# Where the ones-product over the squares stands in PE's order, in a two-layer diffusion trunk on one core

## The chip, the core and the metric

One core of a Trainium2 chip runs the whole program. The time is device microseconds from launch to end. Three timed runs of the kernel before gave 2468.21, 2466.99 and 2468.08 us, a median of 2468.08.
## What is computed

Two trunk layers run over 512 latent and 128 context tokens, 640 in all, with a model width of 1024:

```
mod = silu(cond) @ w_ada + b_ada;  sh1, sc1, g1, sh2, sc2, g2 = split(mod, 6)
h = rms_norm(x, norm1_g) * (1 + sc1) + sh1
z = h @ w_in                       # then four parallel mixers (two attentions, two gated scans)
x = x + g1 * (merged branches @ w_out)
h2 = rms_norm(x, norm2_g) * (1 + sc2) + sh2
x = x + g2 * conv_ffn(h2, w_up, conv_w, conv_b, w_down)
```

`rms_norm` divides each token by the root of the mean of its squares over the 1024 channels. The change touches the two norms only, and the way each is reached from the product in front of it.

## The kernel before

**Layout and precision.** Activations lie transposed: 8 tiles of 128 channels by 640 tokens, x in `XT`. A product in near-fp32 precision is made of three fp32r products: weights and activations are each split into a rounded part (`WHI`, `HH`) and a rest (`RING_split`, `HL`), and `block_product` (lines 795 to 801) issues hi times hi, hi times lo and lo times hi, each in two halves of 320 columns. ACT makes the rounded part of each block of weights (`out_unit`, `up_unit`, `down_unit`, `unit_hi`), DVE the rest (`out_lo`, `up_lo`, `down_lo`, `lo_z`). Every engine's program is written out by hand in its own block, in order; nothing but semaphores couples them. An instruction that waits holds everything behind it on its engine.

**Stages of a layer.** Norm 1, the input projection, the mixers, the merge, the output projection (8 output tiles, `G_OUT` + t, 8 products of 48 matmuls each), norm 2, the up projection with the convolution, the down projection (8 output tiles, `G_DOWN` + j, 132 matmuls each in two parts of 66, over one `Fori` loop of two passes of four tiles on PE), then norm 1 of the next layer.

**How a norm is reached.** For each output tile DVE adds the residual into x (`residual`, line 2411), ACT squares that tile (`square`, line 1378), and DVE adds the square into `SQ_SUM` (`add_square`, line 1986). The first seven squares go into `SQ_SUM`, the eighth stays apart. PE then multiplies both by a matrix of 1/1024 in plain fp32 (`mean_square`, through `wide`, lines 787 and 788): a first pair of matmuls reads `SQ_SUM`, a second pair, added onto it in the same PSUM buffer, reads the eighth square. ACT takes the inverse root with a Ln and an Exp (`inv_root`, lines 1370 and 1372). DVE's `normed` and ACT's `modulate` then make the eight tiles of h in turn: DVE scales a tile (2045 or 2042), ACT rounds it with the shift (1389, and for odd tiles 1398), DVE makes the rest (2032 or 2029, in `rest(k)`). PE's next product (`two_products`, which makes two output tiles at once, 12 matmuls per tile of h) takes the tiles as they come (`h_ready`).

**Late modulation.** The last four column blocks of `w_ada` in a layer are multiplied after the output projection: `late(n)` on PE (line 1209), a copy of each row by ACT (`late_row_out`, line 1794), a turn into columns on PE (`late_turn`, line 1217), and one addition on DVE (line 2435). In `normed` DVE does tiles 0 to 3, then that addition, then tiles 4 to 7.

**The next layer's first weights.** At the sixth output tile of the down projection (j = 6) DVE's list also has `lo_z(l + 1, 0)` and `lo_z(l + 1, 1)` (line 2064), the rests of the next layer's first two weight blocks. They wait for ACT's `unit_hi` (line 1417), and ACT waits with that for the first part of the last output tile (`EV_DOWN + 14`), since the block is written over weights which that part reads.

Of the kernel before, what the change touches and what calls it, by code (L numbers as in the profile page):

```python
# [8 lines left out]
ALU = mybir.AluOpType  # L9
# [280 lines left out]
def build(nc, A, O):  # L290
    ctx = ExitStack()
    with ctx:
# [476 lines left out]
        def _(pe):  # L769
# [3 lines left out]
            for l in range(DEPTH):  # L773
# [63 lines left out]
                def mean_square(which):  # L837

                    if which:
                        wait_taken(pe, l, G_OUT + 6)  # L840
                    elif l:
                        wait_taken(pe, l - 1, G_DOWN + 6)
                    n = 2 * l + which
                    pe.wait_ge(sq_added, 8 * n + 7)
                    wide(pair(MS_AT[n]), ONES, SQ_SUM, True, False)
                    pe.wait_ge(sq_ready, 8 * n + 8)
                    wide(pair(MS_AT[n]), ONES, SQ[1], False, True).then_inc(ms_ready, 1)

                mean_square(0)
# [350 lines left out]

                for t in range(8):
                    wait_room(pe, l, G_OUT + t)
                    lo_ready(U_OUT + t)
                    product(use(G_OUT + t)[0], *out_weights(t), m_hi, m_lo, KT, t % 2 == 0, None if t else m_ready)
# [17 lines left out]
                late(0)  # L1222
                late(1)
                mean_square(1)
# [100 lines left out]
                with pe.Fori(0, 2) as it:  # L1325
                    down_first(it)
                    for j in range(1, 4):
                        g = G_DOWN + j
                        wait_room(pe, l, g, it)
                        for h in range(2):  # L1330
                            lo_ready(U_DOWN + 2 * j + h, it * 8)
                            product(use(g)[0], *down_weights(2 * j + h), lambda k: D_HI[11 * h + k],
                                    lambda k: ZT_R[:, 11 * h + k, :], 11, True, None, h == 0, h == 1)

        @block.scalar
        def _(act):
# [17 lines left out]
            for l in range(DEPTH):  # L1354
# [418 lines left out]
                for t in range(8):  # L1773
                    wait_event(act, l, EV_OUT + t)
                    if t < 5:
                        out_unit(t + 3)
                    elif t == 5:
                        log_and_exp()
                        up_unit(0, 0, w=W_APART)
                    elif t == 7:  # L1780
                        up_unit(0, 1)
                    if t:
# [144 lines left out]
        def _(v):  # L1927
# [12 lines left out]
            for l in range(DEPTH):  # L1940
# [78 lines left out]
                def normed(which, first, last):  # L2019
# [18 lines left out]
                    for k in range(first, last):  # L2038
# [11 lines left out]
                        if k > first:  # L2050
                            rest(k - 1)
                    rest(last - 1)
# [364 lines left out]
                for k in range(KT):  # L2417
                    if k < 5:
                        out_lo(k + 3)
                    elif k == 5:  # L2420
                        up_lo(0, 0, w=W_APART)
                    wait_event(v, l, EV_OUT + k)
# [3 lines left out]
                    if k:  # L2426
# [5 lines left out]
                up_lo(1, 0)  # L2432
                normed(1, 0, 4)
                v.wait_ge(late_turned, l * 4 + 4)
                nv.tensor_tensor(MOD[:, 40:48, :], columns(LATE_COLUMNS, 0, 8), bc(COLS[:, C_BADA + 40:C_BADA + 48].rearrange("p (j o) -> p j o", o=1), 2),
                                 ALU.add).then_inc(late_mod, 1)
                v.wait_ge(late_mod, l + 1)
                normed(1, 4, 8)
# [110 lines left out]
                for j in range(KT):  # L2549
                    if j < KT - 1:  # L2550
                        down_lo(2 * j + 2)
                        down_lo(2 * j + 3)
                    wait_event(v, l, EV_DOWN + 2 * j + 1)
                    residual(G_DOWN + j, j, 40)
                    if l + 1 < DEPTH:
# [5 lines left out]
                        if j:  # L2561
# [110 lines left out]
```

## Time and profile before

| | |
|---|---|
| median of three timed runs | 2468.08 us |
| the profiled execution | 2467.62 us, span 2465.8 us |
| PE busy, share of span | 2367.4 us, 96% |
| DVE, ACT, POOL busy | 1488.1, 1016.8, 305.7 us |
| mean granted TensorE clock | 0.990 |

The profiled execution lies inside the range of the timed runs. Its own time is 1.8 us more than its span. PE is the engine whose time is nearly the whole span; what the other engines do costs something only where PE waits for it, which is in a few places, two of them in each layer in front of a norm's product. In the rows below a line of the timeline begins with the start in us from the span's start and the duration; "x2" says that two instructions in a row were merged; the brackets give how long the engine had been idle and whose instruction ended that. Consecutive instructions of DVE and ACT overlap in the records by about 0.1 us.

### The profile page before, as it was taken

The numbers are of one execution on the slowest core, as the hardware profiler recorded it, in microseconds if no ns is written. First come the engines' busy times: TensorE is split into PE (matmuls) and PEld (weight loads), VectorE is DVE, ScalarE is ACT, GpSimd is POOL, SyncE is SP. The second block draws the span as 40 slices with busy tenths as digits, with TensorE's granted clock in tenths as the row PEclk, the third lists the DMA queues.
The fourth block names the chain that finished last, engine by engine and source line by source line (L and its number), as shares of the span: only waits on it lengthen the run. The fifth ranks groups of instructions, "written<-read, shape, count | busy, mean of one in ns | idle before, by whom it ended". The sixth has DMA issues, their size and how long they took to land. (4 is left out here: it accounts for less than half of the span.)

```text
span 2465.8 us, 49600 instructions
## 1 busy us (share of the span) xinstructions
PE 2367.4 (96%) x21594; PEld 2209.7 (90%) x21594; DVE 1488.1 (60%) x2274; ACT 1016.8 (41%) x1408; POOL 305.7 (12%) x203
## 2 busy tenths in 40 slices
PE   5999999999999999999989999999999999999998
PEld 4999867888999899999989996688899989999998
DVE  4134476986744788883241436778775658888621
ACT  4245565222252555561243536642222544555410
POOL 0000000000000545530000000000000006555000
PEclk8999999999999999999999999999999999999999
DMA  8555211222245233333244431122222633332321
GB/s 274 184 175 167 59 31 49 55 55 55 64 144 180 80 86 86 85 104 91 75 145 129 120 103 52 33 55 54 56 59 81 219 93 85 86 86 75 104 80 66
DMA packets 326509, 239.32 MB, mean 97 GB/s; under 512 B 18272, under 2 KB 317344, under 8 KB 325024
## 3 DMA queue, kind: packets, MB, share of 16 engines
q1 hardware_dynamic: 317584, 211.32, 29.4%
q10 hardware_dynamic: 8720, 24.99, 3.0%
q8 instruction: 162, 2.65, 0.4%
q14 instruction: 43, 0.35, 0.0%
HBM read 220.68 MB, written 15.60 MB: 96 GB/s over the span
## 5 line engine op out<-in xcount | busy, mean ns | idle before, releaser
L798 PE MATMUL PS<-HH_split,WHI_split 128*128 128x320 f32 x1952 | 617.6, 316 | 11.0 <-DVE HL_split L2032 9.5
L800 PE MATMUL PS<-HH_split,RING_split 128*128 128x320 f32 x1920 | 595.7, 310 | 0.0
L799 PE MATMUL PS<-HL_split,WHI_split 128*128 128x320 f32 x1760 | 546.9, 311 | 0.0
L798 PEld LDWEIGHTS PS<-HH_split,WHI_split 128*128 128x128 f32 x1952 | 369.5, 189 | 22.9 <-issue 13.3
L2057 DVE TENSOR_TENSOR RING_split<-RING,WHI_split 128x1024 fp32r<-128x1024 f32 (+2 forms) x154 | 222.4, 1446 | 269.1 <-ACT WHI_split L1725 182.0
L800 PEld LDWEIGHTS PS<-HH_split,RING_split 128*128 128x128 f32 x1920 | 362.7, 189 | 0.0
L799 PEld LDWEIGHTS PS<-HL_split,WHI_split 128*128 128x128 f32 x1760 | 333.7, 190 | 0.3
L799 PE MATMUL PS<-ZT_split,WHI_split 128*128 128x320 f32 x1032 | 320.0, 310 | 0.0
L748 POOL TENSOR_TENSOR BIG<-HH_split,HL_split 128x640 f32<-128x640 f32 x8 | 14.3, 1822 | 1752.9 <-DVE HL_split L2029 1752.9
L2064 DVE TENSOR_TENSOR RING_split<-RING,WHI_split 128x1024 fp32r<-128x1024 f32 x52 | 62.2, 1223 | 229.6 <-ACT WHI_split L1417 229.2
L799 PEld LDWEIGHTS PS<-ZT_split,WHI_split 128*128 128x128 f32 x1032 | 194.7, 189 | 0.0
L1251 PE MATMUL PS<-BIG_split,WHI_split 128*128 128x320 f32 x576 | 178.0, 309 | 0.0
L798 PE MATMUL PS<-V_split,WHI_split 128*128 128x320 f32 x480 | 151.0, 315 | 2.0 <-DVE RING_split L2057 2.0
L800 PE MATMUL PS<-V_split,RING_split 128*128 128x320 f32 x488 | 151.5, 310 | 0.0
L1725 ACT ACTIVATE WHI_split<-RING 128x1408 fp32r<-128x1408 f32 x32 | 44.1, 1379 | 219.7 <-PE PS L800 167.6
L1250 PE MATMUL PS<-V_split,WHI_split 128*128 128x320 f32 x432 | 133.7, 309 | 0.0
L1661 ACT ACTIVATE WHI<-PS 128x640 f32<-128x640 f32 x48 | 33.8, 705 | 223.6 <-PE PS L800 223.2
L1575 ACT ACTIVATE BIG<-PS,NMX 128x768 f32<-128x768 f32 (+1 forms) x120 | 94.2, 791 | 62.8 <-DVE NMX L2160 62.8
L1251 PEld LDWEIGHTS PS<-BIG_split,WHI_split 128*128 128x128 f32 x576 | 108.1, 188 | 0.0
L2263 DVE COPY_PREDICATED BIG<-MASK,PS 128x640 f32<-128x640 uint8 x96 | 84.6, 881 | 34.8 <-PE PS L1130 34.6
L2160 DVE TENSOR_REDUCE NMX<-PS 128x1 f32<-128x768 f32 (+1 forms) x120 | 93.1, 817 | 18.7 <-PE PS L1013 14.5
L1624 ACT ACTIVATE WHI_split<-RING 128x1280 fp32r<-128x1280 f32 (+1 forms) x54 | 67.0, 1241 | 67.9 <-PE PS L800 67.9
(321 smaller groups left out, 5489.6 us busy)
## 6 DMA issues: line engine op xcount, KB each, us to landing
RING<-in_w_in SPq DMA_DIRECT2D x96, 512.0 KB, 4.0
RING<-in_w_up SPq DMA_DIRECT2D x88, 512.0 KB, 5.0
RING<-in_w_ada SPq DMA_DIRECT2D x80, 512.0 KB, 6.3
RING<-in_w_down SPq DMA_DIRECT2D x32, 384.0 KB, 3.5
RING<-in_w_in SPq DMA_DIRECT2D x40, 256.0 KB, 3.3
RING<-in_w_down SPq DMA_DIRECT2D x32, 320.0 KB, 3.9
RING<-in_w_out SPq DMA_DIRECT2D x16, 512.0 KB, 4.5
ZT<-in_w_ada SPq DMA_DIRECT2D x8, 1024.0 KB, 9.0
```

The costliest lines, as they stand in the source:

```text
L798: release(pe.matmul(out, w_hi, hi[:, a:b], start=begin, stop=False), fresh and a == 0)
L799: pe.matmul(out, w_hi, lo[:, a:b], start=False, stop=False)
L800: ins = pe.matmul(out, w_lo, hi[:, a:b], start=False, stop=end)
L1250: release(pe.matmul(out, w_hi[k], hi[:, k, :], start=not onto and k == 0, stop=False, skip_group_check=onto), fresh and k == 0)
L1251: pe.matmul(out, w_hi[k], lo[:, k, :], start=False, stop=False, skip_group_check=onto)
L1575: act.activation(PROB[g % 3][m][:, 0:n], pair(m)[:, 0:n], ACT.Exp, bias=NMX[:, g % 3, m:m + 1], accum_out=SUMS[:, g % 3, m:m + 1]).then_in ...
L1624: act.activation(W2[m % 2][:, 0:width], RING[:, (MIX + m) % N_SLOT, 0:width], ACT.Copy).then_inc(hi_made, 1)
L1725: act.activation(W_DN[q % 2], RING[:, (DOWN + q) % N_SLOT, 0:11 * P], ACT.Copy).then_inc(hi_made, 1)
L2057: nv.tensor_tensor(rest, value, as_f32(hi), ALU.subtract).then_inc(lo_made, 1)
L2064: nv.tensor_tensor(z_raw(RING_R, l, c, j), z_raw(RING, l, c, j), as_f32(w_z(u, 256 if kind in ("t4", "t1") else P)), ALU.subtract).then_in ...
L2160: nv.tensor_reduce(NMX[:, g % 3, m:m + 1], pair(m)[:, 0:keys(g // NS) * P], AX.X, ALU.max, negate=True).then_inc(nmax_ready, 1)
L2263: ins = nv.copy_predicated(SCORE[:, h], m, ps)
```

## The change

`mean_square` is cut in two: `sum_of_seven(n)` has the first pair of matmuls, `mean_square(n)` the second. In each layer `sum_of_seven` for norm 2 is issued inside the last product of the output projection, in front of its seventh tile of eight; for the next layer's norm 1 it is issued inside the last output tile of the down projection, between its two parts. `late(1)` goes from in front of norm 2's products to behind them. On PE the `Fori` loop of the down projection becomes a Python loop, which writes both passes out (13,692 rows of PE instead of 12,746 in the listing of the program). On ACT and DVE the seventh square and its addition go in front of the wait for the last product; ACT's `up_unit(0, 1)` goes from in front of the last two squares to behind them. On DVE the late addition stands inside an unbroken loop over the eight tiles, behind tile 3's scaling and tile 2's rest, and `up_lo(1, 0)` goes from in front of the norm to behind tile 6's scaling.

```diff
-                def mean_square(which):
-
-                    if which:
-                        wait_taken(pe, l, G_OUT + 6)
-                    elif l:
-                        wait_taken(pe, l - 1, G_DOWN + 6)
-                    n = 2 * l + which
+                def sum_of_seven(n):
+
+                    if n:
+                        wait_taken(pe, l, G_OUT + 6 if n % 2 else G_DOWN + 6)
                     pe.wait_ge(sq_added, 8 * n + 7)
                     wide(pair(MS_AT[n]), ONES, SQ_SUM, True, False)
+
+                def mean_square(n):
                     pe.wait_ge(sq_ready, 8 * n + 8)
                     wide(pair(MS_AT[n]), ONES, SQ[1], False, True).then_inc(ms_ready, 1)
...
+                def seven_within(k):
+                    if k == KT - 2:
+                        sum_of_seven(2 * l + 1)
...
-                    product(use(G_OUT + t)[0], *out_weights(t), m_hi, m_lo, KT, t % 2 == 0, None if t else m_ready)
+                    product(use(G_OUT + t)[0], *out_weights(t), m_hi, m_lo, KT, t % 2 == 0, {0: m_ready, KT - 1: seven_within}.get(t))
...
                 late(0)
+                mean_square(2 * l + 1)
                 late(1)
-                mean_square(1)
...
-                with pe.Fori(0, 2) as it:
+                for it in range(2):
...
                             lo_ready(U_DOWN + 2 * j + h, it * 8)
+                            if (it, j, h) == (1, 3, 1) and l + 1 < DEPTH:
+                                sum_of_seven(2 * l + 2)
...
                 for t in range(8):
+                    if t == KT - 1:
+                        wait_taken(act, l, G_OUT + t - 1)
+                        park(t - 1)
+                        square(2 * l + 1, t - 1)
                     wait_event(act, l, EV_OUT + t)
...
                 square(2 * l + 1, KT - 1)
                 park(KT - 1)
+                up_unit(0, 1)
...
+                normed(1, 0, 8, {3: late_modulation, 6: lambda: up_lo(1, 0)})
...
+                    if j == KT - 1 and l + 1 < DEPTH:
+                        add_square(2 * l + 2, j - 1)
                     wait_event(v, l, EV_DOWN + 2 * j + 1)
                     residual(G_DOWN + j, j, 40)
...
-                        if j:
+                        if 0 < j < KT - 1:
                             add_square(2 * l + 2, j - 1)
                         if j == 6:
                             lo_z(l + 1, 0)
```

DVE at the end of layer 0's down projection, before. The rows are the addition of the sixth square, the two rests of the next layer's weights, the residual of the last tile, the addition of the seventh square, and the third rest, in whose waits the eighth square is counted:

```order
L1986 TENSOR_TENSOR WORK<-WORK 128x640 [waits sq_added,sq_ready]
L2064 TENSOR_TENSOR RING_split<-RING,WHI_split 128x8x128 [waits hi_made] x2
L2411 SCALAR_TENSOR_TENSOR BIG<-PS,MOD,BIG 128x512 [waits pe_done]
L2411 SCALAR_TENSOR_TENSOR BIG<-PS,MOD,BIG 128x128
L1986 TENSOR_TENSOR WORK<-WORK 128x640 [waits sq_added,sq_ready]
L2064 TENSOR_TENSOR RING_split<-RING,WHI_split 128x8x128 [waits gemm_free1,gemm_free0,gemm_free2,gemm_free3,sq_ready,sq_added,hi_made]
```

The same place after the change:

```order
L1996 TENSOR_TENSOR WORK<-WORK 128x640 [waits sq_added,sq_ready]
L2076 TENSOR_TENSOR RING_split<-RING,WHI_split 128x8x128 [waits hi_made] x2
L1996 TENSOR_TENSOR WORK<-WORK 128x640 [waits sq_added,sq_ready]
L2423 SCALAR_TENSOR_TENSOR BIG<-PS,MOD,BIG 128x512 [waits pe_done]
L2423 SCALAR_TENSOR_TENSOR BIG<-PS,MOD,BIG 128x128
L2076 TENSOR_TENSOR RING_split<-RING,WHI_split 128x8x128 [waits gemm_free1,gemm_free0,gemm_free2,gemm_free3,sq_ready,sq_added,hi_made]
```

The seventh square's addition moved in front of the last residual, and it stands behind the two rests.

PE at the end of layer 0's down projection, before: the last matmul, the loop's end, and the two pairs of the ones-product:

```order
L800 MATMUL PS<-HL_split,RING_split 128x320
L1325 REGISTER_ALU
L1325 COMPARE_AND_BRANCH
L787 MATMUL PS<-WORK,CONST 128x512 [waits sq_added,gemm_free0]
L788 MATMUL PS<-WORK,CONST 128x128
L787 MATMUL PS<-WORK,CONST 128x512 [waits sq_ready]
L788 MATMUL PS<-WORK,CONST 128x128
```

After the change the first pair stands between the two parts of the last output tile; this is that place, and 66 matmuls of the second part follow the pair:

```order
L799 MATMUL PS<-ZT_split,WHI_split 128x320
L800 MATMUL PS<-HL_split,RING_split 128x320
L787 MATMUL PS<-WORK,CONST 128x512 [waits sq_added,gemm_free0,lo_made]
L788 MATMUL PS<-WORK,CONST 128x128
L798 MATMUL PS<-HL_split,WHI_split 128x320
L799 MATMUL PS<-ZT_split,WHI_split 128x320
```

The wait for `sq_added`, the count of added squares, now stands in front of those 66 matmuls; the second pair alone is left behind them.

PE in front of norm 2 of layer 0, before: the last matmul of the output projection, `late(0)` and `late(1)` as 16 matmuls, the two pairs, and the first turn:

```order
L800 MATMUL PS<-CACHE_split,RING_split 128x320
L1209 MATMUL PS<-ZT,SC 32x256 [waits gemm_free2,late_in]
L1209 MATMUL PS<-ZT,SC 32x256 x15
L787 MATMUL PS<-WORK,CONST 128x512 [waits sq_added,gemm_free0]
L788 MATMUL PS<-WORK,CONST 128x128
L787 MATMUL PS<-WORK,CONST 128x512 [waits sq_ready]
L788 MATMUL PS<-WORK,CONST 128x128
L1217 MATMUL PS<-SEL,WORK 128x2 [waits late_row,gemm_free1]
```

The same place after the change:

```order
L800 MATMUL PS<-CACHE_split,RING_split 128x320
L1214 MATMUL PS<-ZT,SC 32x256 [waits gemm_free2,late_in]
L1214 MATMUL PS<-ZT,SC 32x256 x7
L787 MATMUL PS<-WORK,CONST 128x512 [waits sq_ready]
L788 MATMUL PS<-WORK,CONST 128x128
L1214 MATMUL PS<-ZT,SC 32x256 x8
L1222 MATMUL PS<-SEL,WORK 128x2 [waits late_row,gemm_free1]
```

`late(1)`, the second group of eight, now comes behind the eighth square's pair; the first pair stands 12 matmuls ahead of the last one shown. ACT's order from there on is as before: the copies of the rows of `late(0)` and `late(1)`, `up_unit(1, 0)`, and then the inverse root.

## Rows read from the trace of the kernel before

**Rows 1.** Waits of PE, whole span: line, releaser, total us, times, longest

```profile
PE PS L787 <- DVEq L1984: 18.1, 2, 16.1
```

**Rows 2.** Timeline of PE where the down projection's second pass begins, layer 0

```profile
1173.18 0.31 PE L800 MATMUL PS<-HL_split,RING_split 128*128 128x320 f32 x1
1173.33 0.31 PE L1315 MATMUL PS<-V_split,WHI_split 128*128 128x320 f32 x1
```

**Rows 3.** Timeline of PE from layer 0's last product to layer 1's first

```profile
1250.78 0.31 PE L800 MATMUL PS<-HL_split,RING_split 128*128 128x320 f32 x1
1253.02 1.10 PE L787 MATMUL PS<-WORK,CONST 128*128 128x512 f32 x2 [1.93 <-DVEq L1984]
...
1254.32 1.92 PE L787 MATMUL PS<-WORK,CONST 128*128 128x512 f32 x2
...
1261.55 0.60 PE L798 MATMUL PS<-HH_split,WHI_split 128*128 128x320 f32 x1 [4.89 <-DVE HL_split L2032]
```

**Rows 4.** Timeline of DVE over the last tile of that down projection

```profile
1235.64 0.81 DVE L1986 TENSOR_TENSOR WORK<-WORK 128x640 f32<-128x640 f32 x1
1242.54 2.36 DVE L2064 TENSOR_TENSOR RING_split<-RING,WHI_split 128x1024 fp32r<-128x1024 f32 x2 [6.08 <-ACT WHI_split L1417]
...
1252.06 0.82 DVE L1986 TENSOR_TENSOR WORK<-WORK 128x640 f32<-128x640 f32 x1
```

**Rows 5.** Timeline of ACT over the same stretch

```profile
1235.76 0.74 ACT L1378 ACTIVATE WORK<-BIG 128x640 f32<-128x640 f32 x1 [1.99 <-DVE BIG L2411]
1241.45 2.01 ACT L1417 ACTIVATE WHI_split<-RING 128x1024 fp32r<-128x1024 f32 x2 [4.94 <-PE PS L800]
...
1252.17 0.74 ACT L1378 ACTIVATE WORK<-BIG 128x640 f32<-128x640 f32 x1
1256.70 0.79 ACT L1370 ACTIVATE WORK<-PS,EPSC 128x640 f32<-128x640 f32 x1 [3.79 <-PE PS L788]
```

**Rows 6.** PE's clock by stretches: us, busy (matmuls), granted clock, DMA

```profile
811.00:814.40 3.40, 3.40 (x22) 1.00 0.43 123
...
1261.50:1267.60 6.10, 6.05 (x23) 0.50 0.97 332
...
2015.30:2018.50 3.20, 3.16 (x12) 0.50 0.31 87
```

**Rows 7.** Timeline of PE in front of norm 2, layer 0

```profile
800.61 1.93 PE L1209 MATMUL PS<-ZT,SC 128*32 128x256 f32 x32
803.41 1.10 PE L787 MATMUL PS<-WORK,CONST 128*128 128x512 f32 x2 [0.86 <-DVE WORK L1986]
...
804.56 1.02 PE L787 MATMUL PS<-WORK,CONST 128*128 128x512 f32 x2
...
811.00 0.39 PE L798 MATMUL PS<-HH_split,WHI_split 128*128 128x320 f32 x1 [1.43 <-DVE HL_split L2032]
```

**Rows 8.** Timeline of ACT in front of and within norm 2, layer 0

```profile
802.94 0.64 ACT L1794 ACTIVATE WORK<-PS 128x256 f32<-128x256 f32 x2
803.47 1.05 ACT L1721 ACTIVATE WHI_split<-RING 128x1024 fp32r<-128x1024 f32 x1
805.85 0.80 ACT L1370 ACTIVATE WORK<-PS,EPSC 128x640 f32<-128x640 f32 x1 [1.32 <-PE PS L788]
...
808.81 1.00 ACT L1389 ACTIVATE HH_split<-WORK,MOD 128x512 fp32r<-128x512 f32 x2
...
813.62 1.20 ACT L1389 ACTIVATE HH_split<-WORK,MOD,A 128x512 fp32r<-128x512 f32 x2 [0.72 <-DVE WORK L2042]
...
817.94 1.01 ACT L1389 ACTIVATE HH_split<-WORK,MOD 128x512 fp32r<-128x512 f32 x2 [2.03 <-DVE WORK L2045]
```

**Rows 9.** Timeline of DVE in front of and within norm 2, layer 0

```profile
800.72 1.01 DVE L2411 SCALAR_TENSOR_TENSOR BIG<-PS,MOD,BIG 128x512 f32<-128x512 f32 x2 [5.07 <-PE PS L800]
...
807.44 1.02 DVE L2045 SCALAR_TENSOR_TENSOR WORK<-BIG,A,WORK 128x512 f32<-128x512 f32 x2 [1.55 <-ACT WORK L1372]
...
825.10 0.82 DVE L2029 TENSOR_TENSOR HL_split<-BIG,HH_split 128x640 fp32r<-128x640 f32 x1 [1.44 <-ACT BIG L1398]
```

More of the change, by code:

```diff
@@ L835, in ada_turn @@
                     last.then_inc(ada_done, 1)
-                def mean_square(which):
-                    if which:
-                        wait_taken(pe, l, G_OUT + 6)
-                    elif l:
-                        wait_taken(pe, l - 1, G_DOWN + 6)
-                    n = 2 * l + which
+                def sum_of_seven(n):
+                    if n:
+                        wait_taken(pe, l, G_OUT + 6 if n % 2 else G_DOWN + 6)
                     pe.wait_ge(sq_added, 8 * n + 7)
                     wide(pair(MS_AT[n]), ONES, SQ_SUM, True, False)
+                def mean_square(n):
                     pe.wait_ge(sq_ready, 8 * n + 8)
                     wide(pair(MS_AT[n]), ONES, SQ[1], False, True).then_inc(ms_ready, 1)
-                mean_square(0)
+                if l == 0:
+                    sum_of_seven(0)
+                mean_square(2 * l)
                 def first_turn(a):
@@ L1779, in _ @@
                         up_unit(0, 0, w=W_APART)
-                    elif t == 7:
-                        up_unit(0, 1)
-                    if t:
+                    if 0 < t < KT - 1:
                         wait_taken(act, l, G_OUT + t - 1)
@@ L2017, in modulation_next, with normed @@
                     gains(A1[:], MOD[:, 8:16, :], C_N1)
-                def normed(which, first, last):
+                def normed(which, first, last, between={}):
                     gain, shift = ((A1, 0), (A2, 24))[which]
@@ L2051, in normed @@
                             rest(k - 1)
+                        if k in between:
+                            between[k]()
                     rest(last - 1)
@@ L2421, in _ @@
                         up_lo(0, 0, w=W_APART)
+                    if k == KT - 1:
+                        add_square(2 * l + 1, k - 1)
                     wait_event(v, l, EV_OUT + k)
@@ L2425, in _ @@
                     residual(G_OUT + k, k, 16)
-                    if k:
+                    if 0 < k < KT - 1:
                         add_square(2 * l + 1, k - 1)
@@ L2431, in _, with late_modulation @@
                 up_lo(0, 1)
[L2432 to L2438, printed above, removed]
+                def late_modulation():
+                    v.wait_ge(late_turned, l * 4 + 4)
+                    nv.tensor_tensor(MOD[:, 40:48, :], columns(LATE_COLUMNS, 0, 8), bc(COLS[:, C_BADA + 40:C_BADA + 48].rearrange("p (j o) -> p j o", o=1), 2),
+                                     ALU.add).then_inc(late_mod, 1)
+                    v.wait_ge(late_mod, l + 1)
+                normed(1, 0, 8, {3: late_modulation, 6: lambda: up_lo(1, 0)})
                 def taps(j, h):
```

## Prediction

> **What bounds the kernel now.** I read the page's table first: PE is busy for 96% of the span, so a change pays or costs only where PE stops or runs slowly. Next come PE's waits: among the longest is the ones-product's wait for the count of squares, 18.1 us in two places, of which 16.1 is the start of the program, which the change leaves alone, and the rest is the hole between the layers [rows 1]. Then the timelines of the three places where the ones-product is moved.
>
> Between the layers the last matmul of the down projection starts at 1250.78, PE is idle for 1.93 us, the first pair starts at 1253.02, the second at 1254.32, and after 4.89 us more PE starts layer 1 at 1261.55 [rows 3]. The clock belongs to it: from 1261.5 to 1267.6 PE was granted half, the 1.2 GHz level [rows 6]. In front of norm 2, PE does the late products from 800.61, waits 0.86 us for the seventh square's addition, has the pairs at 803.41 and 804.56, and starts the up projection at 811.00, held by DVE's rest of the first tile [rows 7].
>
> **Between the layers: a wait in the middle of a product.** The first pair now stands between the two parts of the last output tile and waits for the seventh square to be added. The square itself is early: ACT makes it at 1235.76 [rows 5]. But DVE's list has its addition behind the two rests of the next layer's weights, and these wait for ACT's rounding, which starts at 1241.45 because it waits for the first part of that same tile [rows 4, 5]. So PE reaches its wait at the moment at which the chain starts that will end it. The rests run from 1242.54 for 2.36 us, to 1244.90 [rows 4]; the addition takes 0.81, to 1245.7 [rows 4]; PE's second part, 66 matmuls at 0.147 us (0.15 between two starts in [rows 2]) in front of the start at 1250.78, began at 1241.25. With 0.1 us for the signal that is 4.55 us in which PE stands still, with 66 matmuls queued behind the wait and, behind them, the residual, the eighth square and the whole norm. Then the pair itself, 1.15 us (803.41 to 804.56 [rows 7]), which stood in the hole before and now stands in the product.
>
> What the hole gives back: the second pair needs only the eighth square, which ACT starts at 1252.17 and ends at 1252.91, 0.1 us from where the first pair started before [rows 3, 5]. So the second pair starts some 1253.0 on the old scale and takes 1.2 instead of the 3.6 us of both, and the Ln that stood at 1256.70 [rows 5] comes 2.4 us sooner. That is the gain as long as the second pair runs at full clock, and as long as the first product of layer 1 starts as slowly as before. If the pair falls into half clock, the gain is 1.2 (its 1.15 us doubles); if that product loses its half-rate stretch, it is up to 3.8.
>
> The clock after the new stop is not in the trace, so I bound it. At half rate 23 matmuls took 6.05 us where 0.147 each is 3.4, a loss of 2.7; in front of layer 1's norm 2, 12 took 3.16 us, a loss of 1.4; and in layer 0, the same code after the same 1.43 us of idle ran at full clock at once, a loss of nothing [rows 6, 7]. Ends are therefore 0 and 2.7, with up to 1.15 more for a pair at half rate. The nearest row by idle time is the one after 4.89 us, which lost 2.7; the hole there came on top of another, so I take 2.0.
>
> The Trainium skill, "TensorE: Matmul & The Clock Gate", Part 1, says that the throttled state is the default and that activity releases it, and that the monitor is free-running and doesn't reset when a kernel starts. By that rule a stop of this length is followed by half rate for certain, the term is at least the 1.4 above and never 0, and it differs from run to run; the sum by it is the one that I make.
>
> Sum between the layers: 4.55 + 1.15 + 2.0 - 2.4 = +5.3 us.
>
> **Norm 2, twice.** Inside the output projection the first pair costs PE 1.15 us and no wait: the seventh residual is added one product (some 7 us) earlier, and ACT and DVE are idle then (5.07 us in front of the last residual [rows 9]). So the last product ends 1.15 later, and its residual goes from 800.72 to 801.87 and ends at 802.88 [rows 9]. The eighth square follows at once, 0.74 us [rows 5], to 803.6; the second pair 803.7 to 804.85. Before, the Ln could start at 805.85, so this alone would gain 1 us. But `late(1)` now stands behind that pair on PE, and ACT's copy of its row still stands in front of the inverse root on ACT, with a block of weights between them. So: `late(1)`, half of 1.93 [rows 7], to 805.8; the copy, half of 0.64, to 806.15; the weights, 1.05, to about 807.15; then the Ln [rows 8]. It comes 1.3 us later than before, and the wait for the mean of squares, which ended last, gives its place to the wait for `late(1)`. What queues behind it on ACT is the inverse root and all eight roundings, and DVE and PE wait for these.
>
> The scaling of tile 0 started 1.59 us after the Ln (807.44) and takes 1.02 [rows 8, 9], so ACT's first rounding goes from 808.81 to 809.76: +0.95, since before it also had two copies in its way. The late addition inside the loop takes away a break: ACT waited 2.03 us for tile 4's scaling, where in the unbroken pattern it waits 0.72 [rows 8]: -1.3. `up_lo(1, 0)` had been hidden in DVE's wait for the root (1.55 us idle [rows 9]) and now stands in front of tile 7's scaling; 1.18 us, half of the 2.36 of the same shape [rows 4], and its cover is gone, because ACT waits for that scaling: +1.18. The last rest, which started at 825.10 [rows 9], starts 0.85 later. PE's first product waits for it: its eight steps of 12 matmuls need 14.1 us from 811.00, which ends before that rest does. So +0.85 in each layer, and a half-rate stretch at the start of that product disappears in the same slack. Bounds for a layer: -0.9 (the copy doesn't hold the root, `up_lo` half hidden) and +1.4 (the pair or `late(1)` at half rate). Together +1.7.
>
> **The loop written out.** The second pass began 0.15 us after the last matmul of the first [rows 2], the ordinary distance, so nothing is there to gain: 0. [...]
>
> **Sum.** 5.3 + 1.7 = +7.0 us on the profiled execution's 2467.62, which is 2474.6; that execution lies 0.46 under the median, so I predict 2474.8.
>
> **Rivals.**
>
> 1. *The seventh sum is there in time and PE doesn't stop.* For it: the square is 5.5 us early. Against it: DVE's list. It would decide if the rests ran before 1241. Then 1.15 - 2.4 + 1.7 = +0.45, 2468.1, no slower than before.
> 2. *The stop is there, and the clock gives it back.* The new stop costs no half rate (as in layer 0's 811.00), and layer 1 then starts at full rate because its hole is 2.4 us shorter: 4.55 + 1.15 - 3.8 + 1.7 = +3.6, 2471.2. For it: the same code ran at both levels. Against it: the stop is longer than any but the one of 4.89, which lost most.
> 3. *The norms gain after all*, at their lower bound: 5.3 - 1.8 = +3.5, 2471.1. Against it: ACT runs strictly in its order.
> 4. *The clock falls twice*, the pair in the stop and the second pair both at half rate: 4.55 + 1.15 + 3.85 - 1.2 + 1.7 = +10, 2477.7.
>
> **How the numbers follow.** Some 0.2%, 4.9 us, is what a measurement here can tell from no change, so faster is below 2463.2 and slower above 2473.0. The forecast has 0.65, rival 4 0.14, rivals 2 and 3 together 0.14, rival 1 0.04, and 0.03 is for all of the gains at once (no stop, full clock, both norms at their lower bound), 2463 or so. Slower is the forecast, of which I leave 0.02 under the bound, and rival 4 and a little of 2 and 3 mixed with a worse clock: 0.80. Same is 0.17, faster 0.03. The range is 2471.2 to 2477.8: it has rivals 2 and 4 at its ends.
>
> **What would show it.** In the changed kernel's timeline: the first pair at some 1246, with an idle of 4 to 5 us ended by DVE's addition, between the two parts of the last tile; PE's clock at half behind it; a single pair in the hole behind the product, and the Ln some 3.2 us after the last matmul's end instead of 5.6; in norm 2 ACT's inverse root started late by the copy of `late(1)`'s row and not by the pair; ACT's wait of 2 us at tile 4 gone, and one at tile 7 in its place. The forecast is wrong if that stop is under 2 us, or if the Ln of norm 2 follows the second pair at once.

## The result and the profile after

The changed kernel took 2480.21 us, the median of six executions (2474.36 to 2480.88), beside 2467.68 for the kernel before: a ratio of 1.0044 (1.0031 to 1.0057), that is +10.9 us (7.7 to 14.1). It is slower, and by more than the +7.0 forecast. The profiled execution took 2479.9 us with a span of 2478.1, 12.3 more than before; its mean granted clock was 0.986.

Between the layers, PE's timeline of the changed kernel (start, duration, engine, line, operation; the brackets give the idle time before and what ended it) answers to [rows 3]:

```profile
1245.58 0.31 PE L800 MATMUL PS<-HL_split,RING_split 128*128 128x320 f32 x1
1250.26 2.04 PE L787 MATMUL PS<-WORK,CONST 128*128 128x512 f32 x2 [4.37 <-DVE WORK L1996]
1252.10 0.63 PE L788 MATMUL PS<-WORK,CONST 128*128 128x128 f32 x2
1252.38 0.61 PE L798 MATMUL PS<-HL_split,WHI_split 128*128 128x320 f32 x1
...
1263.34 0.31 PE L800 MATMUL PS<-HL_split,RING_split 128*128 128x320 f32 x1
1265.51 2.02 PE L787 MATMUL PS<-WORK,CONST 128*128 128x512 f32 x2 [1.87 <-ACT WORK L1385]
...
1272.85 0.60 PE L798 MATMUL PS<-HH_split,WHI_split 128*128 128x320 f32 x1 [4.89 <-DVE HL_split L2042]
```

PE now stands for 4.37 us in the middle of the last output tile. DVE's timeline shows what it waits for (L2076 the two rests of the next weights, L1996 the seventh addition, as [rows 4]):

```profile
1247.02 2.36 DVE L2076 TENSOR_TENSOR RING_split<-RING,WHI_split 128x1024 fp32r<-128x1024 f32 x2 [6.08 <-ACT WHI_split L1424]
1249.29 0.82 DVE L1996 TENSOR_TENSOR WORK<-WORK 128x640 f32<-128x640 f32 x1
```

The windows of PE in the changed kernel (us, busy and matmuls, granted clock, DMA share, GB/s) show the clock: the first pair and the start of part 2 at half, the rest of part 2 at full, then the second pair and the start of layer 1 at half, each fall behind a pause:

```profile
1250.30:1255.30 5.00, 5.00 (x15) 0.50 0.20 43
1255.40:1263.50 8.10, 8.10 (x56) 1.00 0.28 98
1265.60:1267.90 2.30, 2.30 (x4) 0.50 0.00 0
1272.80:1275.80 3.00, 2.95 (x11) 0.50 1.12 389
```

What the place costs is read by aligning ACT: its rounding of the next layer's weights in front of the place (1241.45 before [rows 5], 1245.93 now, so 4.48 late already), and its first read of layer 1's first product behind it. That read in the kernel before, then in the changed one:

```profile
1277.78 0.70 ACT L1520 ACTIVATE ZT<-PS 128x640 f32<-128x640 f32 x1 [3.47 <-PE PS L800]
```

```profile
1287.69 0.70 ACT L1527 ACTIVATE ZT<-PS 128x640 f32<-128x640 f32 x1 [2.09 <-PE PS L800]
```

It is 9.92 late there (from the unrounded starts), so the place costs 9.92 - 4.48 = 5.44 us.

Norm 2 of layer 0, ACT's timeline of the changed kernel (L1385 a square, here the sixth, which the change doesn't touch; L1804 the copies of late rows, L1728 `up_unit`, L1377 the Ln, L1396 the roundings), as [rows 8]:

```profile
795.87 0.74 ACT L1385 ACTIVATE WORK<-BIG 128x640 f32<-128x640 f32 x1 [4.44 <-PE PS L800]
...
807.91 0.38 ACT L1804 ACTIVATE WORK<-PS 128x256 f32<-128x256 f32 x1 [1.25 <-PE PS L1214]
808.19 1.05 ACT L1728 ACTIVATE WHI_split<-RING 128x1024 fp32r<-128x1024 f32 x1
809.14 0.79 ACT L1377 ACTIVATE WORK<-PS,EPSC 128x640 f32<-128x640 f32 x1
...
810.60 0.67 ACT L1804 ACTIVATE WORK<-PS 128x256 f32<-128x256 f32 x2
811.78 1.01 ACT L1396 ACTIVATE HH_split<-WORK,MOD 128x512 fp32r<-128x512 f32 x2 [0.51 <-DVE WORK L2055]
...
818.80 1.00 ACT L1396 ACTIVATE HH_split<-WORK,MOD 128x512 fp32r<-128x512 f32 x2
...
825.59 1.20 ACT L1396 ACTIVATE HH_split<-WORK,MOD,A 128x512 fp32r<-128x512 f32 x2 [1.86 <-DVE WORK L2052]
```

The same square as in the first row began at 794.05 in the kernel before, so 1.82 us had gathered by then:

```profile
794.05 0.74 ACT L1378 ACTIVATE WORK<-BIG 128x640 f32<-128x640 f32 x1 [4.44 <-PE PS L800]
```

DVE's last rest of the norm (L2039) in the changed kernel is 2.81 later than in [rows 9]; L2069 is `up_lo(1, 0)`, now inside the norm:

```profile
823.60 1.22 DVE L2069 TENSOR_TENSOR RING_split<-RING,WHI_split 128x1024 fp32r<-128x1024 f32 x1
...
827.91 0.83 DVE L2039 TENSOR_TENSOR HL_split<-BIG,HH_split 128x640 fp32r<-128x640 f32 x1 [1.43 <-ACT BIG L1405]
```

Norm 2 therefore costs 2.81 - 1.82 = 0.99; in layer 1 the same alignment gives 0.99.

The two places make 5.44 + 1.98 = 7.4 us of the 12.3. The other 4.9 arise outside these places, and 1.82 of them before the first instruction that the change moves. The largest piece is in layer 1, in code that is the same in both programs. From PE's first matmul behind one pause there to a matmul behind the next, the same work took 33.6 us before and 36.3 in the changed kernel, 2.7 more. PE's timeline of the kernel before, then of the changed one:

```profile
1496.48 1.13 PE L1011 MATMUL PS<-ZT 32*128 32x512 f32 x4 [1.26 <-ACT BIG L1575]
...
1530.09 0.42 PE L978 MATMUL PS<-HH_split,RING_split 128*128 128x320 f32 x1
```

```profile
1506.40 1.13 PE L1012 MATMUL PS<-ZT 32*128 32x512 f32 x4 [1.26 <-ACT BIG L1582]
...
1542.66 0.41 PE L979 MATMUL PS<-HH_split,RING_split 128*128 128x320 f32 x1
```

PE's windows at about the same code (columns as above), before and then after, show the reason: behind both pauses the clock was at full before and is at half now.

```profile
1498.50:1501.50 3.00, 2.45 (x19) 1.00 0.00 0
1529.00:1532.00 3.00, 3.00 (x36) 1.00 0.00 0
```

```profile
1508.20:1511.00 2.80, 2.61 (x12) 0.50 0.04 14
1538.80:1541.80 3.00, 3.00 (x22) 0.50 0.12 47
```

### The profile page after: what moved, and what is told of

The parts are those of the page before. It is cut to its first block and busy times, and to the rows that moved or that the text cites. A ratio compares the mean times of both kernels' runs of the same rounds, so it can differ in the third digit from the quotient of the medians.

```text
span 2478.1 us, 49560 instructions
## 1 busy us (share of the span) xinstructions
PE 2375.5 (96%) x21594; PEld 2216.5 (89%) x21594; DVE 1488.3 (60%) x2274; ACT 1016.8 (41%) x1408; POOL 305.6 (12%) x203
## 5 line engine op out<-in xcount | busy, mean ns | idle before, releaser
L798 PE MATMUL PS<-HH_split,WHI_split 128*128 128x320 f32 x1952 | 617.6, 316 | 10.9 <-DVE HL_split L2042 9.4
L2069 DVE TENSOR_TENSOR RING_split<-RING,WHI_split 128x1024 fp32r<-128x1024 f32 (+2 forms) x154 | 222.7, 1447 | 272.8 <-ACT WHI_split L1732 182.5
L2076 DVE TENSOR_TENSOR RING_split<-RING,WHI_split 128x1024 fp32r<-128x1024 f32 x52 | 62.2, 1223 | 227.0 <-ACT WHI_split L1424 225.9
```

What stands on the lines that cost most here:

```text
L798: release(pe.matmul(out, w_hi, hi[:, a:b], start=begin, stop=False), fresh and a == 0)
L2069: nv.tensor_tensor(rest, value, as_f32(hi), ALU.subtract).then_inc(lo_made, 1)
L2076: nv.tensor_tensor(z_raw(RING_R, l, c, j), z_raw(RING, l, c, j), as_f32(w_z(u, 256 if kind in ("t4", "t1") else P)), ALU.subtract).then_in ...
```

## Experiments

Each ran beside the kernel before on the same chip. In the table "between" and "norm 2" are the costs of the places against the profiled execution of the kernel before, by aligning ACT as above (norm 2 to ACT's first read of the up projection). "Pauses" is what the stretch of layer 1 just shown took beyond the 33.6 us of the kernel before. "us" is the ratio times 2468.

| kernel | median us | ratio (interval) | us | between | norm 2, per layer | pauses |
|---|---|---|---|---|---|---|
| changed | 2480.21 | 1.0044 (1.0031 to 1.0057) | +10.9 | 5.44 | 1.00, 0.99 | 2.7 |
| changed, again | 2476.14 | 1.0032 (1.0020 to 1.0045) | +7.9 | 3.65 | 0.99, 0.99 | 2.7 |
| early addition | 2469.51 | 1.0005 (0.9996 to 1.0014) | +1.2 | -1.60 | 0.99, 0.98 | 2.7 |
| loop written out | 2468.24 | 1.0001 (0.9992 to 1.0010) | +0.2 | -1.80 | -0.01, 0.01 | 0.0 |
| between only | 2476.64 | 1.0039 (1.0025 to 1.0052) | +9.6 | 3.96 | -0.01, -0.01 | 2.7 |
| norm 2 only | 2468.68 | 1.0005 (0.9996 to 1.0014) | +1.2 | 0.03 | 1.00, 1.02 | 0.0 |
| root first | 2474.69 | 1.0031 (1.0019 to 1.0043) | +7.7 | 3.94 | 0.79, 0.80 | 2.7 |
| early addition, root first, `up_lo` late | 2468.07 | 1.0000 (0.9991 to 1.0009) | 0 | -2.53 | -0.34, -0.17 | 2.7 |
| stop longer | 2481.38 | 1.0060 (1.0047 to 1.0074) | +14.8 | 7.20 | 0.99, 0.99 | 2.7 |
| stop filled | 2469.83 | 1.0013 (1.0004 to 1.0023) | +3.2 | 1.91 | 1.00, 0.99 | 2.7 |
| norm sooner, early addition | 2466.95 | 0.9985 (0.9976 to 0.9994) | -3.7 | -2.65 | -1.76, -0.22 | 2.6 |
| norm sooner alone | 2466.33 | 0.9989 (0.9980 to 0.9998) | -2.7 | -1.86 | -0.22, -0.22 | 0.0 |
| rows first | 2468.27 | 1.0000 (0.9991 to 1.0009) | 0 | -1.60 | -1.30, -1.28 | 2.7 |

The last column splits the kernels cleanly. All ten traces with the first pair inside the product pay 2.6 to 2.7 us at the two pauses of layer 1, with a stop or without one. The four with the pair behind the product (the kernel before, loop written out, norm 2 only, norm sooner alone) pay nothing. So this goes with the move of the pair, and neither with the stop nor with the written-out loop; it rests on one traced execution of each kernel, and why the clock falls there isn't shown.

**Early addition.** The changed kernel with the seventh addition in front of DVE's rests:

```diff
-                    if j == KT - 1 and l + 1 < DEPTH:
-                        add_square(2 * l + 2, j - 1)
...
                         if j == 6:
+                            add_square(2 * l + 2, j)
                             lo_z(l + 1, 0)
```

> The changed kernel with the seventh square's addition put in front of the two rests of the next layer's weights on DVE, nothing else. Theory A (the stop): the 4.4 us of idle between the two parts of the last tile go, and with them the half-rate stretch behind it (2.3 us); between the layers +0 to -2 against the kernel before instead of +5.4; the norms keep their +1.0 each, so some 2468 to 2470 at the median, 6 to 7 us under the changed kernel in executions of a like clock. Theory B (the written-out loop costs 5 us by itself, wherever it shows): still 5 us over that, some 2474. Rival C (the stop is not what costs, it is covered): no difference to the changed kernel's 2480 or 2474.5.

PE's timeline has the pair in the product without a pause:

```profile
1244.36 0.31 PE L800 MATMUL PS<-HL_split,RING_split 128*128 128x320 f32 x1
1244.51 1.02 PE L787 MATMUL PS<-WORK,CONST 128*128 128x512 f32 x2
1245.37 0.38 PE L788 MATMUL PS<-WORK,CONST 128*128 128x128 f32 x2
```

With the stop gone, the time falls from 2480.21 to 2469.51: nearly all of the loss hangs on the order of one addition of 0.82 us.

**Loop written out.** The kernel before with `Fori` replaced.

```diff
-                with pe.Fori(0, 2) as it:
+                for it in range(2):
```

> The kernel before with PE's loop over the down projection written out, nothing else. Theory A: no difference to the kernel before (2467.7), within 0.1%. Theory B: the longer program brings the part of the loss that lies away from the three places, 4.9 us in the profiled execution: 2472.6, with more half-rate stretches of PE's clock than the kernel before has.

No difference. Its trace shows something else. It has the same order between the layers as the kernel before, and yet the place is 1.80 us shorter, 1.24 of them because the second pair ran at full rate (PE, where [rows 3] had 1.92 us for the second pair) and the rest in layer 1's first product:

```profile
1256.00 1.10 PE L787 MATMUL PS<-WORK,CONST 128*128 128x512 f32 x2 [1.93 <-DVEq L1984]
1256.93 0.38 PE L788 MATMUL PS<-WORK,CONST 128*128 128x128 f32 x2
1257.16 1.02 PE L787 MATMUL PS<-WORK,CONST 128*128 128x512 f32 x2
```

Its Ln, in ACT's timeline, comes 2.44 us behind the first pair's start; in the kernel before it was 3.68 (1253.02 to 1256.70):

```profile
1258.44 0.80 ACT L1370 ACTIVATE WORK<-PS,EPSC 128x640 f32<-128x640 f32 x1 [2.54 <-PE PS L788]
```

**Between only, and norm 2 only.** The changed kernel with all edits at norm 2 undone, and the kernel before with those edits alone; the diffs are the two halves of the change.

> The changed kernel with everything at norm 2 put back (ones-product behind the output projection, late modulation in the break, ACT's and DVE's order); the move between the layers and the written-out loop stay. Theory A: +5.4 between the layers and nothing else, 2473, give or take 3 for where the clock's half-rate stretches fall. Theory B: 5.4 + 4.9, 2478 in most executions.

> The kernel before with only the part at norm 2 changed; the loop is still a loop and the ones-product between the layers stands behind the down projection. Theory A: +1.0 in each layer, 2469.7. Rival D (the profiled execution's +1.0 is the clock's doing and the order gains): under 2467. Theory B has nothing to add here: 2469.7.

+9.6 and +1.2 add up to the changed kernel's +10.9. Norm 2 costs 1.0 a layer, as in the whole. Between only lies 3.6 us above Theory A's 2473; 2.7 of its time are at the two pauses of layer 1, and Theory B's loop isn't the cause, since alone it costs nothing.

**Stop longer.** Three idle subtractions on DVE in front of the seventh addition.

```diff
+                        for _ in range(3):
+                            step.mark(nv.tensor_tensor(HL_R[:, 7, :], XT[:, 0, :], XT[:, 0, :], ALU.subtract))
+                            step.settle(v)
                         add_square(2 * l + 2, j - 1)
```

> The changed kernel with three idle subtractions of 640 columns on DVE in front of the seventh addition between the layers (0.82 us each in the rows of DVE, with the waits between them some 3 us), so PE stands at the first pair some 7.4 us instead of 4.37. Theory A (the stop costs its length, and beside it a fixed fall of the clock behind it: the pair 0.97 us and part 2 some 1.35 us slower): the clock has already fallen after 4.4 us, so 3 us more of standing cost 3 us: the whole some 3 us above the changed kernel's 2480.2, or 2482 to 2484. Rival E (what the program pays beyond the 7.4 us read at the changed places comes from this stop, since a longer stop moves the clock's stretches of everything behind it): no proportion, anywhere from 2475 to 2488, and the pauses behind the stop fall to half rate at other places. Rival F (the first pair's wait lies beside other waits later): no change, 2480.

PE stood 6.95 us, 2.58 more:

```profile
1248.17 2.05 PE L787 MATMUL PS<-WORK,CONST 128*128 128x512 f32 x2 [6.95 <-DVE WORK L1996]
```

Against the second trace of the changed kernel (3.65), which has the same full-rate second pair, the place costs 3.55 more: 2.58 of standing, 0.6 because part 2 ran at half rate for longer (about as long as in the first trace), and 0.3 in layer 1's first product. The pair takes the same 2 us: the half rate isn't deeper behind a longer stop. By the ratios the whole is 3.9 above the first batch of the changed kernel and 6.9 above the second, with intervals of some 3 us each. Theory A's 3 is near what the place shows. Rival F falls; the times alone don't exclude Rival E.

**Stop filled.** The wait stays, and PE multiplies a finished tile into the pair's place meanwhile.

```diff
+                    if n and n % 2 == 0:
+                        for _ in range(4):
+                            wide(pair(MS_AT[n]), ONES, XT[:, 0, :], True, True)
                     pe.wait_ge(sq_added, 8 * n + 7)
```

> The changed kernel with four further pairs of matmuls (ones by a finished tile of x, into the pair's own place in PSUM, overwritten by the pair that follows) in front of the wait for the seventh addition, so PE works 4.6 us where it stood 4.37 us; nothing of the result uses them. Theory A: part 2 still begins as late (0.2 us later), but the clock stays at 2.4 GHz: the first pair takes 1.15 us instead of 2.12 and part 2 gives back some 1.35 us: 2.1 us below the changed kernel, 2477 to 2478.5. Rival E (all that the changed kernel pays beyond the places it touches hangs on PE's idleness here): 5 to 7 us below, 2473 to 2475. Rival G (the clock is set by something else than PE's idle time here): the pair still takes 2 us, and the time is as the changed kernel's or 0.2 us above.

PE's timeline: the pair starts as late behind part 1 as before (4.4 us), but at full clock, and so does part 2:

```profile
1248.71 1.02 PE L787 MATMUL PS<-BIG,CONST 128*128 128x512 f32 x2
1249.57 0.39 PE L788 MATMUL PS<-BIG,CONST 128*128 128x128 f32 x2
1249.91 1.12 PE L787 MATMUL PS<-WORK,CONST 128*128 128x512 f32 x2
1250.87 0.39 PE L788 MATMUL PS<-WORK,CONST 128*128 128x128 f32 x2
```

The place costs 1.91 though the addition comes no sooner: 1.74 less than in the second trace of the changed kernel, whose second pair ran at full rate as it does here, where Theory A had 2.1. The whole falls by 7.7 us against the first batch and by 4.7 against the second (by the ratios), each give or take some 4: nearer Rival E's 5 to 7, with Theory A's 2.1 inside the second alone. One comparison is cleaner. Nine of the eleven executions lie between 2469.2 and 2472.2, but the traced one took 2476.2, and outside the place its clock falls at the same code as in the first trace of the changed kernel, all through. Between these two alike executions the whole differs by 3.7 us and the place by 3.5, so nothing beyond the place is gained there, as Theory A has it; why most executions are shorter still is open. Rival G falls: work that nothing uses made the program faster, because PE wasn't idle. Two of the falls elsewhere (PE's windows, where the columns are as above):

```profile
262.20:265.00 2.80, 2.80 (x12) 0.50 0.73 193
422.60:425.00 2.40, 2.40 (x10) 0.50 0.00 0
```

**Root first.** ACT's inverse root in front of `late(1)`'s row.

```diff
                 late_row_out(0)
+                inv_rms(1)
                 late_row_out(1)
                 up_unit(1, 0)
-                inv_rms(1)
```

> The changed kernel with ACT's inverse root of norm 2 in front of the copy of late(1)'s row and of up_unit(1, 0), instead of behind both. In the changed kernel the copy waited 1.25 us for late(1) and the inverse root began at 809.14 though the pair had long ended. Theory A: the root begins some 2 us earlier, and the last rest of norm 2 comes 1 to 2 us earlier in each layer: 2 to 3.5 us below the changed kernel, and norm 2 then shorter than in the kernel before. Rival D (the norm's length is set by DVE's turns with ACT's roundings, and the delayed copies only shift the wait): norm 2 as long as in the changed kernel, no change of the whole.

ACT's timeline: the Ln comes 2.2 us sooner (0.37 of drift deducted here, 1.82 above), but the first rounding only 0.2.

```profile
805.44 0.79 ACT L1377 ACTIVATE WORK<-PS,EPSC 128x640 f32<-128x640 f32 x1 [0.22 <-PE PS L788]
...
809.86 0.38 ACT L1804 ACTIVATE WORK<-PS 128x256 f32<-128x256 f32 x1 [0.48 <-PE PS L1214]
810.14 1.00 ACT L1396 ACTIVATE HH_split<-WORK,MOD 128x512 fp32r<-128x512 f32 x2
```

What is late next are the copies of the rows of `late(2)` and `late(3)`, which stand in front of the roundings and wait for PE. My expectation of 2 us was wrong here.

**Early addition, root first, `up_lo` late.** Also `up_lo(1, 0)` behind the norm:

```diff
-                normed(1, 0, 8, {3: late_modulation, 6: lambda: up_lo(1, 0)})
+                normed(1, 0, 8, {3: late_modulation})
+                up_lo(1, 0)
```

> The changed kernel with three edits: the seventh addition between the layers in front of DVE's two rests (that alone measured 2469.5), ACT's inverse root of norm 2 first, and DVE's up_lo(1, 0) behind the norm instead of in it. Theory A: no stop; norm 2 shorter by 2 us (root) and up to 1 us (DVE's 1.22 us rest no longer ahead of tile 7) in each layer: 4 to 6 us below 2469.5, so 2463.5 to 2466, below the kernel before. Rival D (norm 2 is bound by DVE's turns): 2468 to 2469.5.

Norm 2 falls from 0.8 to -0.3 and -0.2: `up_lo(1, 0)` at tile 6 is worth 1.0 to 1.1 a layer, the forecast's 1.18. The whole is level with the kernel before, not 2 to 4.5 us below it as expected: the places gain 3.0 us, and the two pauses of layer 1 take 2.7.

**Norm sooner, with and without the early addition.** ACT's `up_unit(1, 0)` and DVE's rest of it go into the pause behind tile 6, `up_unit(0, 1)` in front of the eighth square, and the last two copies among the roundings:

```diff
                         square(2 * l + 1, t - 1)
+                        up_unit(1, 0)
...
                 late_row_out(0)
+                inv_rms(1)
                 late_row_out(1)
-                up_unit(1, 0)
-                inv_rms(1)
-                late_row_out(2)
-                late_row_out(3)
                 for k in range(KT):
                     modulate(1, k, A2, 24)
+                    if k < 2:
+                        late_row_out(k + 2)
```

> The changed kernel with the seventh addition between the layers in front of DVE's two rests (measured alone: 2469.5), and norm 2 rearranged: ACT makes up_unit(1, 0) and DVE its rest in the gap that both have behind tile 6 (7.06 us of ACT, 5.11 us of DVE in the trace with the root first), up_unit(0, 1) stands in front of the eighth square, the inverse root in front of late(1)'s row, and the copies of the rows of late(2) and late(3) behind the first and second rounded tile. In the trace with the root first, DVE had the first tile at 808.4 and ACT took it at 810.59, held by those copies and by up_unit. Theory A (norm 2 is set by what ACT does between the eighth square and the first rounding): the first rounding 2.1 us sooner, the last rest about as much, 4 us over both layers: 2463 to 2465.5. Rival D (norm 2 is bound by the turns of ACT and DVE, so an earlier start comes to nothing): 2467 to 2469.5.

> The kernel before with norm 2 alone as in the rearranged version, and nothing changed between the layers. Theory A: norm 2 alone costs 1 us a layer in the changed kernel and gains 2 us over the one with the root first: 3 to 5 us below the kernel before. Against the version with both, it tells whether the pair of seven inside part 2 without a stop gains or costs: Theory A says between -1 and +1 us. Rival D: as the kernel before.

Both are below the kernel before: 0.9985 (0.9976 to 0.9994) and 0.9989 (0.9980 to 0.9998). The first lies between what Theory A (2463 to 2465.5) and Rival D (2467 to 2469.5) expected. They don't tell whether the pair inside the product gains without a stop. PE's timeline of the first shows the new bound of norm 2:

```profile
812.18 0.61 PE L1222 MATMUL PS<-SEL,WORK 128*128 128x2 f32 x4 [1.54 <-ACT WORK L1806]
812.65 0.39 PE L798 MATMUL PS<-HH_split,WHI_split 128*128 128x320 f32 x1
```

Its last rest began at 823.66, but the product of 14.1 us begins only behind the turn of `late(3)`'s row, so it ends after 826 and has become the bound. Norm 2 gains 1.76 us there. In layer 1, and in both layers of the other version, the start of that product ran at half rate behind the same pause, and only 0.2 is left.

**Rows first.** `late_row_out(3)` in front of the second rounding.

```diff
-                    if k < 2:
-                        late_row_out(k + 2)
+                    if k == 0:
+                        late_row_out(2)
+                        late_row_out(3)
```

> The rearranged version (2466.95) with the copy of late(3)'s row in front of the second rounded tile instead of behind it. In its trace the last rest of norm 2 in layer 0 began at 823.66, 1.4 us earlier than in the kernel before though 0.7 us of drift had gathered by then, but PE's first product began only at 812.65, held 1.54 us by the turn of that row, and its 96 matmuls at 0.147 us need 14.1 us, to 826.8. Theory A (the sooner norm has made PE's first product the bound of this place, and it waits for the row): the product begins 1.0 to 1.5 us sooner, 1 to 2.5 us over both layers, 2464.5 to 2466. Rival H (ACT's later roundings, 0.3 us late by the copy, set the end): 0 to 0.6 us later than the rearranged version.

PE's first product begins at 810.70, 1.6 us sooner than there (drift deducted), as Theory A had it. But the two copies now delay the roundings: the last rest begins 0.9 later than there and is the bound again, which is Rival H's picture. Norm 2 is 1.3 shorter than before in both layers, 2.6 in all where the version before it had 2.0. The time, expected at 2464.5 to 2466, was level with the kernel before: the places gain 4.2 us by the trace, the two pauses of layer 1 take 2.7, and the 1.5 left is inside the interval.

**The changed kernel again.**

> The changed kernel itself once more, for more executions and a second trace. The sum of what the two places cost by alignment of the traces is 5.4 + 2.0 = 7.4 us, the ratio measured gave 10.9 (7.7 to 14.1). Theory A (the rest is where the clock falls at pauses common to both programs, which varies from one execution to the next): the places again cost 7 to 8 us in the new trace, half-rate stretches elsewhere lie partly at other pauses, and the ratio comes nearer to 7.4: 2475 to 2480. Rival E (the stop itself brings the further falls): the same pauses fall again, and the median stays at 2480.

Two traces of one program, 2479.9 and 2475.4 us. Their difference of 4.5 lies in steps of up to 1.6 us, nearly all at stretches that one ran at half rate and the other didn't. Windows of PE at the same code, first of the one, then of the other:

```profile
262.20:265.00 2.80, 2.80 (x12) 0.50 0.67 179
422.60:425.60 3.00, 3.00 (x12) 0.50 0.00 0
1119.00:1122.00 3.00, 3.00 (x13) 0.50 0.88 274
```

```profile
262.20:265.00 2.80, 2.80 (x21) 1.00 0.67 177
422.60:425.60 3.00, 3.00 (x21) 1.00 0.00 0
1117.50:1120.50 3.00, 3.00 (x22) 1.00 0.86 250
```

The second trace also has the second pair at full rate, which is most of why its place costs 3.65 and not 5.44; so its places cost 5.6 us together, not the 7 to 8 expected. Both traces have the two falls in layer 1. The median fell to 2476.1, as Theory A had it, and did not stay at Rival E's 2480.

## Why the prediction was wrong, step by step

The direction was right, and so were the mechanism and the sum at the changed places: 5.3 + 1.7 forecast, 5.44 + 1.98 in the first trace. The step that failed is the one from these places to the whole. The sum has no term for the rest of the program, which it put at nothing without a reason, and there the runs showed 2.7 us more in layer 1. Against the forecast's terms between the layers, with the two traces of the changed kernel, each set against a trace of the old order whose second pair ran at the rate named (us):

| term between the layers | forecast | first trace, against the kernel before | second trace, against the loop written out |
|---|---|---|---|
| stop and pair at full rate | 4.55 + 1.15 | 5.68 | 5.67 |
| clock behind the stop | 2.0 | 2.38 | 1.63 |
| hole's gain | -2.4 | -1.26 | -1.11 |
| first product of layer 1 | 0 | -1.39 | -0.76 |
| sum | 5.3 | 5.41 | 5.43 |

The first row is the distance from part 1's last matmul to part 2's first (1245.58 to 1252.38), less one matmul of 0.147 and the pair's 0.97 at half rate. The second is that 0.97 and part 2's loss, 1252.38 to 1263.34 against 65 matmuls at 0.147. The third is the distance from the last matmul to the Ln, 4.66 us against 5.92 (1250.78 to 1256.70 [rows 3, 5]); the fourth from the Ln to ACT's read of that product, 19.69 against 21.08. The last column is read in the same way. The sums are the 5.44 and 5.45 of the alignment to 0.03.

- *The rest of the program* is the step that failed. In the ten traces with the first pair inside the product the clock falls behind two pauses of layer 1 and takes 2.6 to 2.7 us; in the four of the old order it doesn't. With it the first trace's places make 7.4 + 2.7 = 10.1 us and the second's 5.6 + 2.7 = 8.3, beside the measured 10.9 (7.7 to 14.1) and 7.9 (4.9 to 11.1).
- *The stop* came where it was forecast, ended by the addition behind DVE's two rests: 4.37 against 4.55. Early addition and stop filled show that it carries most of the loss.
- *What the hole gives back* was mis-sized, and the sum between the layers came out partly by luck. The forecast took the 3.6 us of both pairs from [rows 3] as what the hole costs. But the second pair there, 1.92 us, ran at half rate; of the four traces of the old order norm 2 only has it so too, while in the loop written out and norm sooner alone the same stretch needed 1.2 less. Against a full-rate pair the gain is 1.1, not 2.4. In the first trace the new single pair fell to half rate as well (2.02), so little was given back there too. In both columns layer 1's first product, put at 0, made up for most of that, since a shorter part of it ran at half rate. Rival 4's picture, both pairs at half rate, is what the first trace shows; its +10 is near the measured 10.9, but not for its reason, since the changed places cost 7.4 there.
- *The clock*: 2.0 was taken for the stop's term; it was 2.38 and 1.63. Stop filled shows that it is PE's idle time that costs it. The Trainium skill ("TensorE: Matmul & The Clock Gate", Part 1) states that the monitor runs freely and that the number of slow matmuls varies from run to run. The two traces agree on the variation, at 262 us for one. The forecast drew from it only that the term is not 0, and gave no width to the rest of the program.
- *Norm 2*: 0.99 a layer against 0.85. ACT's wait at tile 4 is gone and one of 1.86 stands at tile 7, as forecast. The copy did hold the root, but root first shows that this is worth only 0.2: behind it the copies of the last two rows hold the first rounding anyway. `up_lo(1, 0)` at tile 6 is worth 1.1. So the sum was right and its first term was named after the wrong copy.
- *The loop written out*: 0, as measured. The whole gave 1.0001 (0.9992 to 1.0010). The Trainium skill ("Runtime: NRT & Kernel Launch", "Instruction fetch mechanics") has a fetch stall at a taken branch whose target lies outside the two pages of instructions at hand. No run here shows whether this branch is of that kind; no stall shows at it, 0.15 us [rows 2].

What stays open is why four of the first six executions lay at 2480 and five of the second six at 2475 to 2477: the other falls of the clock differ between executions. The first trace has some at 262 and 422; stop filled has them at the same code, and so has the loop written out, so these belong neither to the stop nor to the move. Nothing here shows what decides them, nor why moving the pair makes the clock fall at the two pauses of layer 1. (The forecast's last step has a slip of 0.3 besides: 2474.6 and 0.46 are 2475.1, not 2474.8.)

## What to carry to other kernels

A change that shifts PE's pauses can move the clock's falls far from the place that was edited, and its cost is then more than the sum of the edited places: compare the untouched stretches of the two traces too, in more than one variant. Before an interval of the profile is credited as a saving, look at the rate at which its matmuls ran: an interval stretched by a half-rate clock may belong to that execution and not to the kernel. A wait moved from the end of a product into its middle needs the order of the engine that ends it; here one addition behind two others cost nearly everything. And when a stop can't be removed, matmuls that nothing uses may cost less than an idle engine.

## What the runs showed of the hardware

Twelve executions of the changed kernel lay between 2474.4 and 2480.9 us; those around 2480 had a mean granted clock of 0.986, the shorter ones 0.989 to 0.991. Four pairs of matmuls that nothing uses, in a stop of 4.4 us, kept the clock at 2.4 GHz behind it, where it otherwise fell to 1.2 in each of the five traces with the stop. Behind two pauses of 1.26 us in layer 1 the clock fell in ten traces of ten with the first pair inside the product of the layer before, and in none of the other four.
